# Split fp32r products for the query, key and value projections and the even layer's columns, and a new order of requests

## The reference

```python
# stack 1, layer 0: time mix on shifted inputs
xx = x_prev - x
xm = x[None] + xx[None] * mu[:, None, None, :]      # six mixes of x
# stack 1, layer 1: masked attention, 16 heads of 64, causal
q = x @ w_q; k = h @ w_k; v = h @ w_v
p = softmax(q @ k.T * 64 ** -0.5 + causal)
# stack 2, layer 0 (the "even" layer), 256 tokens and 256 of context
cols = h @ w_in                    # neighbourhood q, k, v; mLSTM q/k (4 head pairs), v, output gate; gates
attn = softmax(q @ k.T * 64 ** -0.5 + rpb_bias + window)
```

## Time and profile before

| | us |
|---|---|
| median of 3 runs | 3188.55 |
| lowest, highest | 3182.97, 3189.29 |
| the profiled execution | 3187.2 |
| its span in the trace | 3185.4 |
| PE busy | 2937.7 |
| DVE, ACT busy | 1856.8, 1409.6 |
| PE in the attention's query and key columns (L286) | 57.02 |
| PE in the even layer's columns (L286) | 112.92 |
| DVE's first instruction | 23.16 |

### The profile page before, as it was taken

How to read it: one execution, slowest core, us unless ns; L and a number is a source line. 1 busy time by engine, 2 the same in 40 slices (tenths; PEclk the granted TensorE clock), 3 DMA queues, 4 the chain that set the end, 5 groups by cost and what they waited for, 6 DMA issues and landing times. The chain is left out here.

```text
span 3185.4 us, 38727 instructions
## 1 busy us (share of the span) xinstructions
PE 2937.7 (92%) x15533; PEld 2259.6 (71%) x15533; DVE 1856.8 (58%) x2272; ACT 1409.6 (44%) x1799; POOL 13.5 (0%) x13
## 2 busy tenths in 40 slices
PE   6999899988799999999999989999779999899798
PEld 4799789777576676766767664548667777657796
DVE  3565455425588888888888840215444453445675
ACT  3221244324466766666666641112233333343554
POOL 0000000000000000000000000000000000000000
PEclk9999699999799999999999999999689999999999
DMA  4400365743799989988999973110012222210352
GB/s 158 146 1 1 119 237 182 261 154 112 278 356 356 348 337 346 346 338 347 351 352 347 352 307 118 62 66 4 1 61 93 89 86 90 80 47 14 128 181 103
DMA packets 94031, 585.86 MB, mean 184 GB/s; under 512 B 20400, under 2 KB 21504, under 8 KB 24480
## 3 DMA queue, kind: packets, MB, share of 16 engines
q1 hardware_dynamic: 91920, 580.27, 49.0%
q10 hardware_dynamic: 1936, 3.13, 0.3%
HBM read 582.31 MB, written 1.05 MB: 183 GB/s over the span
## 5 line engine op out<-in xcount | busy, mean ns | idle before, releaser
L2064 DVE TENSOR_TENSOR s_w_low<-weight_ring,s_w_high 128x2048 fp32r<-128x2048 f32 x336 | 759.7, 2290 | 127.1 <-ACT s_w_high L2003 123.3
L2003 ACT ACTIVATE s_w_high<-weight_ring 128x2048 fp32r<-128x2048 f32 x336 | 630.0, 1909 | 128.4 <-PE bank L1984 105.8
L257 DVE TENSOR_TENSOR s_w_low<-weight_ring,s_w_high 128x1024 fp32r<-128x1024 f32 x238 | 289.7, 1222 | 196.1 <-ACT s_w_high L239 195.9
L239 ACT ACTIVATE s_w_high<-weight_ring 128x1024 fp32r<-128x1024 f32 x238 | 250.0, 1052 | 282.2 <-PE bank L533 278.9
L1984 PE MATMUL bank<-s_w_high,s_x_low 128*96 128x512 f32 x896 | 355.9, 397 | 7.6 <-DVE s_w_low L2064 7.6
L533 PE MATMUL bank<-s_x_high,s_w_low 128*128 128x256 f32 (+1 forms) x1056 | 341.8, 324 | 20.0 <-DVE s_x_low L607 14.7
L1984 PE MATMUL bank<-s_w_high,s_x_high 128*96 128x512 f32 x896 | 356.2, 398 | 0.0
L1984 PE MATMUL bank<-s_w_low,s_x_high 128*96 128x512 f32 x896 | 353.8, 395 | 0.0
L533 PE MATMUL bank<-s_x_low,s_w_high 128*128 128x256 f32 (+1 forms) x1056 | 340.4, 322 | 0.0
L533 PE MATMUL bank<-s_x_high,s_w_high 128*128 128x256 f32 (+1 forms) x1056 | 340.2, 322 | 0.0
L533 PEld LDWEIGHTS bank<-s_x_high,s_w_low 128*128 128x128 f32 x1056 | 202.8, 192 | 39.9 <-DVE s_w_low L257 18.5
(11 more groups left out here) (478 smaller groups left out, 4386.2 us busy)
## 6 DMA issues: line engine op xcount, KB each, us to landing
weight_ring<-moe_w SPq DMA_DIRECT2D x336, 1024.0 KB, 6.7
weight_ring<-ada_w SPq DMA_DIRECT2D x48, 1024.0 KB, 6.5
weight_ring<-ffn_up SPq DMA_DIRECT2D x44, 1024.0 KB, 4.8
weight_ring<-ffn_w_in SPq DMA_DIRECT2D x22, 1024.0 KB, 4.9
weight_ring<-ffn_down SPq DMA_DIRECT2D x22, 1024.0 KB, 4.8
weight_ring<-ffn_w_down SPq DMA_DIRECT2D x11, 1024.0 KB, 4.8
weight_ring<-w_rkv_cols SPq DMA_DIRECT2D x8, 1024.0 KB, 8.5
weight_ring<-moba_qk SPq DMA_DIRECT2D x8, 1024.0 KB, 9.8
```

What stands on the lines that cost most here:

```text
L239: K.nc.scalar.activation(self.hi[:, b, :], self.source(c, i), ACT.Copy).then_inc(*self.high.up())
L257: K.nc.vector.tensor_tensor(self.lo[:, b, :], self.source(c, i), self.hi[:, b, :], ALU.subtract)\
L2003: nc.scalar.activation(halves(whi, kind, n, i), raw(kind, n, i), ACT.Copy).then_inc(S["high"].h, 1)
L2064: V.tensor_tensor(halves(wlo, kind, n, i), raw(kind, n, i), halves(whi, kind, n, i), ALU.subtract)\
```

## The change

`constants` takes two functions: SP's eight requests and ACT's four of the front block are made in it, SP's ahead of `c_cols` and the ring. `moba_projections` replaces the two calls in `causal_attention`: one block, in which ACT and DVE split hT once, eight query and key chunks are multiplied in fp32r at depth 2, and the four value chunks follow from the same split input, into other banks; two of the four value copies go to ACT, and the two casts lie ahead of the wait for the last product. `split_cols` replaces `linear_cols` in `even_layer`, at depth 1, with its split buffers laid over units that are still free (the bias table's among them). The six gate tables are asked for ahead of the columns, the 33 requests of the bias and window behind them, in the gates' block, and the bias addition moves behind `peaked` with a wait of its own.

```diff
@@ -167,7 +167,7 @@
-def constants(K):
+def constants(K, ahead, aside):
...
+        @block.scalar
+        def _(act):
+            aside(act)
         @block.sync
         def _(sp):
+            ahead(sp)
             sp.dma_start(K.cond[:, :, :], K.i["c_cols"]).then_inc(*K.early["cond_in"].up(16))
...
@@ -314,6 +319,73 @@
+def split_cols(K, x, jobs, zero, parts_at, x_at):
+    nc = K.nc
+    xhi, xlo = x_at
+    chunks = sum(n for n, _ in jobs)
+    evac, zeroed, xsplit, xlow = K.sig(4)
+    parts = Split(K, None, chunks, 1, bufs=parts_at)
+    bank = lambda c, h: K.ps[c % 3 * 2 + h][:, :]
+    with K.begin() as block:
+        @block.tensor
+        def _(pe):
+            for c in range(chunks):
+                if c >= 3:
+                    pe.wait_ge(*evac.at(c - 2))
+                for i in range(2):
+                    pe.wait_ge(*parts.low.at(2 * c + i + 1))
+                    for h in range(2):
+                        for k in range(KT // 2):
+                            j = i * (KT // 2) + k
+                            if c == h == 0 and j % 2 == 0:
+                                pe.wait_ge(*xlow.at(j // 2 + 1))
+                            at = slice(k * 256 + h * P, k * 256 + h * P + P)
+                            for p, (ws, xs) in enumerate(((parts.lo, xhi), (parts.hi, xlo), (parts.hi, xhi))):
+                                last = nc.tensor.matmul(bank(c, h), ws[:, i, at], xs[:, j, :],
+                                                        start=(j == 0 and p == 0), stop=(j == KT - 1 and p == 2))
+                    last.then_inc(*(K.used if i else parts.half).up())
+                K.taken += 1
...
+        @block.scalar
+        def _(act):
+            parts.act(act, -1)
+            for q in range(0, KT, 2):
+                nc.scalar.activation(xhi[:, q:q + 2, :], x[:, q:q + 2, :], ACT.Copy).then_inc(*xsplit.up())
+            act.wait_ge(*zeroed.at(1))
+            c = 0
+            for n, fn in jobs:
+                for m in range(n):
+                    parts.act(act, c)
+                    act.wait_ge(*K.used.at(c + 1))
+                    for h in range(2):
+                        last = fn(act, m, h, bank(c, h))
+                    K.a(act, last, evac)
+                    c += 1
+        @block.vector
+        def _(dve):
+            parts.dve(dve, -1)
+            for q in range(0, KT, 2):
+                dve.wait_ge(*xsplit.at(q // 2 + 1))
+                nc.vector.tensor_tensor(xlo[:, q:q + 2, :], x[:, q:q + 2, :], xhi[:, q:q + 2, :], ALU.subtract)\
+                    .then_inc(*xlow.up())
+            for c in range(chunks):
+                parts.dve(dve, c)
...
@@ -674,6 +746,18 @@
...
+        def ahead(sp):
+            fetch(sp, "x_loaded", (xT[:, :, :], i["x_cols"]))
+            fetch(sp, "low_loaded", (w1s[:, :, :], i["decay_w1"]), (a1s[:, :, :], i["iclr_a1"]),
+                  (g1s[:, :, :], i["gate_g1"]))
+            fetch(sp, "low2_loaded", (w2s[:, :], i["decay_w2"]), (a2s[:, :], i["iclr_a2"]),
+                  (g2a[:, :], i["gate_g2"][0:P, :]), (g2b[:, :], i["gate_g2"][P:160, :]))
+        def aside(act):
+            fetch(act, "mix_loaded", (mu[:, :, :], i["mu_cols"]), (cols[:, :, :], i["rwkv_cols"]))
+            fetch(act, "masks_loaded", (bones[:, :], i["head_block"]), (hsel[:, :], i["head_pick"]))
+        constants(K, ahead, aside)
         with K.begin() as block:
...
@@ -757,8 +841,6 @@
...
             def _(act):
-                fetch(act, "mix_loaded", (mu[:, :, :], i["mu_cols"]), (cols[:, :, :], i["rwkv_cols"]))
-                fetch(act, "masks_loaded", (bones[:, :], i["head_block"]), (hsel[:, :], i["head_pick"]))
                 fetch(act, "later_loaded", *loads)
...
@@ -876,11 +958,6 @@
...
             def _(sp):
-                fetch(sp, "x_loaded", (xT[:, :, :], i["x_cols"]))
-                fetch(sp, "low_loaded", (w1s[:, :, :], i["decay_w1"]), (a1s[:, :, :], i["iclr_a1"]),
-                      (g1s[:, :, :], i["gate_g1"]))
-                fetch(sp, "low2_loaded", (w2s[:, :], i["decay_w2"]), (a2s[:, :], i["iclr_a2"]),
-                      (g2a[:, :], i["gate_g2"][0:P, :]), (g2b[:, :], i["gate_g2"][P:160, :]))
                 K.stream(sp)
...
@@ -1586,6 +1663,107 @@
...
+def moba_projections(K, x, jobs, zero, vr, late, rounded):
+    nc = K.nc
+    evac, zeroed, xsplit, xlow, kept = K.sig(5)
+    wide = sum(n for n, _ in jobs)
+    chunks = wide + KT // 2
+    with ExitStack() as st:
+        parts = Split(K, st, chunks, 2)
+        K.uniq += 1
+        xhi, xlo = (st.enter_context(nc.sbuf_tensor(f"s{K.uniq}_x_{n}", [P, KT, T], F32R)) for n in ("high", "low"))
+        bank = lambda c, h: K.ps[c % 3][:, h * T:(h + 1) * T]
+        row = lambda tt, h: K.ps[4 + 2 * tt + h][:, :]
+        with K.begin() as block:
+            @block.tensor
+            def _(pe):
+                for c in range(wide):
+                    if c >= 3:
+                        pe.wait_ge(*evac.at(c - 2))
+                    pe.wait_ge(*parts.low.at(2 * c + 1))
+                    for h in range(2):
+                        for j in range(KT):
+                            if h == 0 and j == KT // 2:
+                                pe.wait_ge(*parts.low.at(2 * c + 2))
+                            if c == h == 0 and j % 2 == 0:
+                                pe.wait_ge(*xlow.at(j // 2 + 1))
+                            b, k = parts.at(c, j // (KT // 2)), j % (KT // 2)
+                            at = slice(k * 256 + h * P, k * 256 + h * P + P)
+                            for p, (ws, xs) in enumerate(((parts.lo, xhi), (parts.hi, xlo), (parts.hi, xhi))):
+                                last = nc.tensor.matmul(bank(c, h), ws[:, b, at], xs[:, j, :],
+                                                        start=(j == 0 and p == 0), stop=(j == KT - 1 and p == 2))
+                            if h and j == KT // 2 - 1:
+                                last.then_inc(*parts.half.up())
+                    last.then_inc(*K.used.up())
+                    K.taken += 1
+                for c in range(wide, chunks):
+                    for i in range(2):
+                        pe.wait_ge(*parts.low.at(2 * c + i + 1))
+                        b, j = parts.at(c, i), 2 * (c - wide) + i
+                        for tt in range(TT):
+                            for h in range(2):
+                                n = slice(h * 512, (h + 1) * 512)
+                                for p, (xs, ws) in enumerate(((xlo, parts.hi), (xhi, parts.lo), (xhi, parts.hi))):
+                                    last = nc.tensor.matmul(row(tt, h), xs[:, j, tt * P:(tt + 1) * P], ws[:, b, n],
+                                                            start=(j == 0 and p == 0), stop=(j == KT - 1 and p == 2))
+                        last.then_inc(*(K.used if i else parts.half).up())
+                    K.taken += 1
...
+            @block.scalar
+            def _(act):
+                parts.act_half(act)
+                for q in range(0, KT, 2):
+                    nc.scalar.activation(xhi[:, q:q + 2, :], x[:, q:q + 2, :], ACT.Copy).then_inc(*xsplit.up())
+                parts.act(act, -1)
+                act.wait_ge(*zeroed.at(1))
+                c = 0
+                for n, fn in jobs:
+                    for m in range(n):
+                        parts.act(act, c)
+                        act.wait_ge(*K.used.at(c + 1))
+                        for h in range(2):
+                            last = fn(act, m, h, bank(c, h))
+                        K.a(act, last, evac)
+                        c += 1
+                parts.act(act, chunks)
+                act.wait_ge(*K.used.at(chunks))
+                for h in range(2):
+                    last = nc.scalar.activation(vr[:, 0, h * 512:(h + 1) * 512], row(0, h), ACT.Copy)
+                K.a(act, last, kept)
+            @block.vector
+            def _(dve):
+                parts.dve_half(dve)
+                for q in range(0, KT, 2):
+                    dve.wait_ge(*xsplit.at(q // 2 + 1))
+                    nc.vector.tensor_tensor(xlo[:, q:q + 2, :], x[:, q:q + 2, :], xhi[:, q:q + 2, :], ALU.subtract)\
+                        .then_inc(*xlow.up())
+                parts.dve(dve, -1)
+                for c in range(wide):
+                    parts.dve(dve, c)
+                    if c < 4:
+                        late(dve, c)
+                parts.dve(dve, chunks)
+                rounded(dve)
+                dve.wait_ge(*K.used.at(chunks))
+                for h in range(2):
+                    last = nc.vector.tensor_copy(vr[:, 1, h * 512:(h + 1) * 512], row(1, h))
+                K.v(dve, last)
 def causal_attention(K, hT, h2, h3, turned, loads):
...
@@ -1596,17 +1774,14 @@
...
         one, low = (st.enter_context(K.nc.sbuf_tensor(f"s{K.uniq}_{n}", [P, P], F32R)) for n in ("one", "causal"))
-        with ExitStack() as st1:
```

(47 more changed lines are left out.)

## The result

The changed kernel takes **3140.26 us** (median of 4 runs, 3137.37 to 3145.13) against 3186.51 (4 runs, 3182.97 to 3189.29) for the kernel before: ratio 0.9857, 95% interval 0.984 to 0.9874. Forecast were 3145 and 3136 to 3154. The profiled execution took 3138.99 us, span 3137.2, which is 48.2 us less than the span before.

A forecast was written before the change was run, and what follows sets the result against it. PE, busy 92% of the span, was taken as the chain from the first product on, with a wait for x before it. 14.0 + 13.8 + 15.6 = 43.4 us gave 3145 us, range 3136 to 3154.

The forecast's parts named there:

- Part 1: Start of the kernel: front block's requests made in `constants`, so DVE starts at 9.1 instead of 23.16 us; -14.0 us.
- The 9.1: Front block's opening in us, taken between 8.2 (no hold-up of SP's requests) and 11.9 (same end as now).
- Rival A: Start: a full queue holds SP, front block opens at 11.9 us; gain 40.7 us, 3148; chance 0.12.
- Part 2: Masked attention: query, key and value in one block, query and key products in fp32r; -13.8 us.
- the late second half: Masked attention's first chunk: second half of the weights, split behind four pieces of x, holds PE 0.3 us more.
- Part 3: Even layer's columns: 128 f32 products become 384 in fp32r, halves of 5.6 us; -15.6 us.
- The splits overlap the products: Masked attention and even columns: ACT's 1.05 and DVE's 1.22 us splits are hidden within PE's 5.76 or 5.6 us.
- rival D: Both projections: splits don't overlap products, adding 39.5 and 59 us; 55 us slower, 3243; chance 0.03.
- The bias addition: Gates: DVE's 4.42 us addition moves behind `peaked`, into 26.17 us of idling for PE; cost nothing, 4.4 us without cover.
- The passes: Both projections: three fp32r products take 0.82 of the f32 time by the rows, against 0.75 by the skill's page.
- Rival B: Both projections: three fp32r passes cost 0.75 of f32; gain 11.7 us larger, 3133; chance 0.03.
- Rival C: PE's restarts or later gappy stretches: slow clock gives some back, up to 3 us each; +8 us, 3153; chance 0.08.

The follow-up runs named there:

- the last two kernels: Kernel after, 416-byte pad ahead of the input's parts in the 512-token dense layers: 3135.59 us; with both dense layers' weights' parts moved 128 bytes as well: 3133.86 us.
- `dve_twice`: Kernel after, with DVE making the low part of every half of the even columns' weights twice: 3140.47 us, ratio 0.9857.
- second trace: The kernel before, unchanged, run and profiled once more: 3190.28 us.
- the kernel with the masked attention alone: Kernel before with only `moba_projections` in place of the two old calls: 3175.34 us, ratio 0.996.
- the second traces of both kernels: The kernels before and after, each unchanged and profiled once more: 3190.28 us and 3138.79 us.

## Why the prediction was right

- **Part 1, predicted 14.0 us, was 13.72.** The block opened by SP's last request, as argued; the last request ended at 8.92 us and the block opened 0.5 us later, at 9.4 where 9.1 was put. The 9.1 was a choice between two bounds; the 15 requests took 8.2 us and not 7. Rival A (SP held until 11.9) did not occur: the six ring requests took 3.08 us (3.25 before), and the last two gate requests, which took 3.41 us behind the ring, took 1.09 ahead of it. That a full queue was what held them before is not shown. Nor had the hold-up begun with about 7 MB asked for: by the sizes it was 8.4 MB.
- **Part 2, predicted 13.8 us, was 13.9.** PE started 3.1 us after the opening, chunks took 5.76 us, and there was no gap ahead of the values. Of the 69.9 us from the first product to 676.9, 8 chunks and 96 products of 0.2267 us are 67.8; the 2.1 left are the slow start and the late second half, put at 1.9. The tail was 2.0 us, as put (1.4 and 0.6); the sum has another 0.2 us ahead of it (698.6, then 698.8) without a source.
- **Part 3, predicted 15.6 us, was 18.5.** Head 4.75 (put at 4.85). The first half took 8.24 us, 2.8 more than the others (put at 2.9). The mis-sized term is the half: 5.44 us and not the 5.6 of the earlier trace rows, 16 x 0.16 = 2.6 us. The row was right for its own layer; it held a loss that the even columns don't have, as the last two kernels show. The gain lies at the upper bound, 18.5.
- **The splits overlap the products**, as argued, and `dve_twice` shows it. But the reading against rival D was wrong in one of its two layers: in the dense layer on 512 tokens of the kernel before PE does wait for `s_w_low`, nine times for 0.6 us, where DVE's convolution lies ahead of a split. It did no harm, since DVE has nothing but splits to do in the even columns.
- **The bias addition cost nothing**, ahead of a wait of 23.4 us that is left. The loads had less time than the prediction gave them: SP makes the 33 requests one after the other from 1976.87 to 1999.28, so the last was asked for 40 us ahead of the addition and not over 60. The price without that cover was put at 4.4 us; put back at the start, the addition cost 15, since the loads and not the addition are then waited for.
- **The passes.** Three fp32r products of 512 columns take 3 x 0.2267 = 0.680 us, the f32 product 112.92 / 128 = 0.882 with its slow start: 0.77 to 0.79 of it, by whether the slow start is taken off. With 256 columns it is 0.360 against 0.433 (55.4 / 128), 0.83. The prediction's 0.82 holds with the slow starts taken off on both sides (89.6 of 110, 46.1 of 55.4); the products as it lists them give 0.79 and 0.81. Rival B, the ratio 0.75 that follows from the four passes of the Trainium skill (FP8 and Floating Point Precision, "TensorE Precision Notes"), is not what either shows; of the 7.1 us by which it would have shortened part 3's halves, 2.6 were there, for another reason.
- **Rival C, the clock.** What it names occurred with both signs: 7.5 us came, mostly in the recurrence, and stood in no term; 5.8 went. Of the losses the largest is the gates and the neighbourhood attention, 170.0 us before and 173.4 after. The first 15 us of the gates and a later stretch, after:

```profile
1977.00:1992.00 15.00, 15.00 (x69) 12.93 (x70) 9.86 (x25) 5.87 (x8) 0.00 (x0) 0.58 0.54 150
...
2052.00:2067.00 15.00, 15.00 (x37) 6.58 (x35) 0.00 (x0) 0.00 (x0) 0.00 (x0) 0.92 0.04 17
```

The first 15 us in the kernel before, then in its second trace:

```profile
2031.00:2046.00 15.00, 14.54 (x70) 12.24 (x71) 13.89 (x24) 3.81 (x5) 0.00 (x0) 0.66 0.18 70
```

```profile
2032.00:2047.00 15.00, 15.00 (x69) 12.85 (x70) 13.93 (x24) 4.10 (x6) 0.00 (x0) 0.59 0.15 63
```

The bias loads now run beside the gates (DMA share 0.54, the last but one number, against 0.18), but the loss is there without them too: the second trace of before took 173.4 us as well, and so did the kernel with the masked attention alone, whose gates have the code and the loads of before (0.57 and a DMA share of 0.15). So the change isn't needed for the loss: the kernel before shows both 170.0 and 173.4 us, with the granted clock lower in the longer one. Of the other 2.4 us, 1.7 went in the stage after the neighbourhood attention (175.8 us before, 177.5 after), and the second traces of both kernels, 174.8 and 175.2, don't show it.

The sum, 43.4 us, stands against 46.1 in the three stretches, 48.2 in the two profiled executions and 46.3 in the medians. Of the 4.7 us between the forecast 3145 and the measured 3140.26, 2.0 are the median of before, 3188.55 with three runs and 3186.51 with four. The sum came close with one term 2.6 us too small. What the clock gave and took, 7.5 and 5.8 us, is larger than that and was not foreseen; that it nearly cancels is luck.

## What to carry to other kernels

Cost a stage by the nearest row with the same loop, but ask whether that row has a loss of its own: here a pitch 3% longer than needed, from the operands' places alone. What a faster product is worth has to be read where the stage runs steadily, not in its first chunks: here another engine took back nearly half of it. An addition that is moved together with the requests for its operand should be priced by when the loads are asked for and land, not by its own length. And for a few us that appear where no code differs, the granted clock is read, and a second trace of the kernel before is looked at, before a cause is sought in the change.

## What was not expected of the hardware

A 512-column fp32r product has a pitch of 0.2267 us where the weights' and the moving tensor's parts begin at the same address modulo 512 bytes in SBUF, and 0.2334 where they don't (384 against 480, and 384 against 0). These are the compiled program's addresses. Both equal places that were tried in the dense layer are fast, 384 with 384 and 0 with 0, and each of them is slow beside another, so it isn't the place of one operand alone. Bringing the input's parts to the weights' took the up halves from 5.60 to 5.44 us where PE waits for nothing (in the 44 of them 3.7 us were won), and bringing the weights' to the hidden tensor's took 22 down halves from 5.58 to 5.44. Products of 256 columns show 0.120 us in either case. Only 0, 96 and 128 bytes apart were seen, 0 fast and both others slow, so a smaller modulus that tells them apart (256) is not excluded, and the experts' products, with weights of 96 columns, were not tried. The granted clock in the recurrence, 267 to 276 us for the same code, is the other thing: up to 9 us, against an interval of 5 to 6 us for a ratio of two kernels.
